# The four transposes of an expert's hidden chunk: from one block ahead of the up products to single ones among them

## The reference, cut to what matters

```
def expert_block(args):
    xb, e = args
    return (jax.nn.silu(xb @ w_gate[e]) * (xb @ w_up[e])) @ w_down[e]
```

## Time and profile before

| what | value |
|---|---|
| median of 3 runs | 1530.83 us (1530.35 to 1530.88) |
| the profiled execution's own time | 1531.03 us |
| its span | 1528.9 us |
| PE busy | 1507.9 us, 99% |
| DVE busy | 1261.7 us, 83% |
| ACT busy | 1096.9 us, 72% |
| first and last turn of a chunk | 581.4 us and 1508.0 us |

### The profile page before, as it was taken

How to read it: one execution, slowest core, us unless ns; L and a number is a source line. 1 busy time by engine, 2 the same in 40 slices (tenths; PEclk the granted TensorE clock), 3 DMA queues, 4 the chain that set the end, 5 groups by cost and what they waited for, 6 DMA issues and landing times.

```text
span 1528.9 us, 22186 instructions
## 1 busy us (share of the span) xinstructions
PE 1507.9 (99%) x7296; PEld 1202.8 (79%) x7296; DVE 1261.7 (83%) x1554; ACT 1096.9 (72%) x1379; POOL 25.2 (2%) x21
## 2 busy tenths in 40 slices
PE   8999999999999999999999999999999999999997
PEld 7778888888877777778778777777777777777775
DVE  5568676666577669999999999999999999999997
ACT  6565555555567648788788888878788788788885
POOL 0000000000000000000000000000000000000000
PEclk9999999999999989999999999999999999999999
DMA  9534374555545479999999999999999999999970
GB/s 339 188 113 137 130 254 166 206 205 190 183 162 183 150 275 368 384 368 380 389 374 376 382 376 371 377 387 366 381 392 358 383 390 355 389 389 356 403 274 30
DMA packets 193224, 454.00 MB, mean 297 GB/s; under 512 B 8176, under 2 KB 12144, under 8 KB 192912
## 3 DMA queue, kind: packets, MB, share of 16 engines
q1 hardware_dynamic: 190560, 443.72, 78.6%
q0 software_dynamic: 2608, 9.57, 2.3%
HBM read 447.37 MB, written 5.90 MB: 296 GB/s over the span
## 4 chain that ended last, share of the span: by engine, by line
PE 95%; DVE 2%; ACT 1%; issue 1%; DMA 0%; SPq 0%; ACTq 0%; DVEq 0%
PE bank L296 26%; PE bank L298 26%; PE bank L297 25%; PE bank L1475 6%; PE bank L1477 3%; PE bank L1996 1%; PE bank L366 1%; DVE w_lo L309 1%; PE bank L794 1%; PE bank L1450 0%; PE bank L1296 0%; PE bank L783 0%; PE bank L1764 0%; PE bank L1771 0%; PE bank L1287 0%
## 5 line engine op out<-in xcount | busy, mean ns | idle before, releaser
L309 DVE TENSOR_TENSOR w_lo<-ring_low,w_hi 128x1024 fp32r<-128x1024 f32 (+2 forms) x442 | 532.7, 1216 | 91.1 <-ACT w_hi L305 64.2
L305 ACT ACTIVATE w_hi<-ring_low 128x1024 fp32r<-128x1024 f32 (+2 forms) x442 | 465.6, 1055 | 137.2 <-PE bank L298 129.0
L309 DVE TENSOR_TENSOR w_lo<-ring,w_hi 128x1024 fp32r<-128x1024 f32 x336 | 404.8, 1222 | 40.0 <-ACT w_hi L305 19.4
L305 ACT ACTIVATE w_hi<-ring 128x1024 fp32r<-128x1024 f32 x336 | 354.8, 1062 | 83.3 <-PE bank L298 83.2
L296 PE MATMUL bank<-w_hi,xe_hi 128*128 128x512 f32 x896 | 353.7, 395 | 0.0
L298 PE MATMUL bank<-w_hi,xe_lo 128*128 128x512 f32 x896 | 349.7, 390 | 0.0
L297 PE MATMUL bank<-w_lo,xe_hi 128*128 128x512 f32 x896 | 348.8, 389 | 0.0
L298 PEld LDWEIGHTS bank<-w_hi,xe_lo 128*128 128x128 f32 x896 | 168.2, 188 | 36.0
L296 PEld LDWEIGHTS bank<-w_hi,xe_hi 128*128 128x128 f32 x896 | 168.3, 188 | 34.7
L297 PEld LDWEIGHTS bank<-w_lo,xe_hi 128*128 128x128 f32 x896 | 168.4, 188 | 34.2
L296 PE MATMUL bank<-w_hi,hT_hi 128*96 128x512 f32 x448 | 177.2, 395 | 0.0
(11 more groups left out here) (308 smaller groups left out, 1650.8 us busy)
## 6 DMA issues: line engine op xcount, KB each, us to landing
ring<-m_gate_dram SPq DMA_DIRECT2D x72, 1024.0 KB, 5.4
ring_low<-m_down_dram SPq DMA_DIRECT2D x72, 1024.0 KB, 6.1
ring<-m_up_dram SPq DMA_DIRECT2D x56, 1024.0 KB, 5.5
ring_low<-m_up_dram SPq DMA_DIRECT2D x56, 1024.0 KB, 6.1
ring_low<-m_gate_dram SPq DMA_DIRECT2D x40, 1024.0 KB, 5.7
ring<-m_down_dram SPq DMA_DIRECT2D x40, 1024.0 KB, 5.4
ring_low<-f_gate_dram SPq DMA_DIRECT2D x14, 1024.0 KB, 5.2
ring_low<-f_up_dram SPq DMA_DIRECT2D x14, 1024.0 KB, 6.1
```

Source lines behind the costliest of these rows:

```text
L305: nc.scalar.activation(w_hi[:, buf, 0:width], src, ACT.Copy).then_inc(hi_ready, 1)
L309: nc.vector.tensor_tensor(w_lo[:, buf, 0:width], src, f32(w_hi[:, buf, 0:width]), ALU.subtract).then_inc(split_ready, 1)
```

## The change

The four transposes of `turn(c-1)` no longer stand between the gate and the up products of chunk c. `gate_up("u", c, q, turned=True)` places one behind each of the first four values of k, that is behind the 3rd, 6th, 9th and 12th matmul of the item, and the fourth counts `h_banked` up. The two waits of `turn` stand ahead of the first up product, with the same values. `turn` itself remains for chunk 6. That makes 6 turns in each of 8 experts, 48 in all, with 192 transposes; 8 turns stay as they were.

```
+            def turn_block(c, j):
+                return nc.tensor.transpose(pb[6][:, j * PLACES:j * PLACES + PLACES], eh[c % 2][:, j * P:j * P + P],
+                                           const("ident")[0:PLACES, 0:PLACES])
+
-            def gate_up(kind, c, q, units=slice(0, 4)):
+            def gate_up(kind, c, q, units=slice(0, 4), turned=False):
                 bank = pb[2 * (c % 2) + (kind == "u")]
+                if turned:
+                    pe.wait_ge(e_prod, 7 * q + (c + 1))
+                    if c > 1:
+                        pe.wait_ge(hT_lo_done, 7 * q + (c - 1))
                 for m, u, n, buf in m_units((kind, c))[units]:
...
                         ins = mm3(bank, xe_hi[:, k, :], xe_lo[:, k, :], w_hi[:, buf, w], w_lo[:, buf, w],
                                   k == 0, k == KD - 1)
+                        if turned and k < 4:
+                            block = turn_block(c - 1, k)
+                            if k == 3:
+                                block.then_inc(h_banked, 1)
                     ins.then_inc(unit_used, 1)
...
                     gate_up("g", c, q)
-                    turn(c - 1, q)
...
-                    gate_up("u", c, q)
+                    gate_up("u", c, q, turned=True)
```

More of the change, by code:

```diff
@@ L1995, in turn @@
                 for j in range(4):
-                    ins = nc.tensor.transpose(pb[6][:, j * PLACES:j * PLACES + PLACES], eh[c % 2][:, j * P:j * P + P],
-                                              const("ident")[0:PLACES, 0:PLACES])
+                    ins = turn_block(c, j)
                 ins.then_inc(h_banked, 1)
```

## The result

The changed kernel takes 1575.93 us (median of 4 runs, 1575.22 to 1576.4), the kernel before 1530.86 us in the same series (4 runs, 1530.35 to 1531.31). The ratio is 1.0294 with a 95% interval of 1.0282 to 1.0307. The forecast was 1575.

A forecast was written before the change was run, and what follows sets the result against it. PE, busy for 99%, was taken as the bound, with ACT and DVE feeding it through four buffers. 1531.03 + 42.2 (transposes and hand-over) + 2.2 (later waits) = 1575.4, stated as 1575 us, range 1560 to 1592.

The forecast's parts named there:

- Part 1: PE's up item: each single transpose costs 0.12 us, four 0.48 instead of the block's 0.36; 5.8 us in all.
- The rival by which the next load would be pulled ahead of the transpose: PE's weight loads: each single transpose costs only 0.04 us, time 1563 us; chance 0.10.
- Part 2: Turned chunk's hand-over from PE to ACT and DVE: PE waits 0.76 us before down; with transposes 0.88 a turn, 42.2 us.
- E: Moment in each turn when the gate item ends and the next product could start on PE; forecast times count from it.
- Part 3: Later waits on DVE's work, at the picks, `turn(LAST)` and the last expert: together 2.2 us.
- the rival that would have kept it at 1.34: DVE's "d" units stay at ACT's pace, 1.34 us apart instead of 1.13: 14 us more, 1589 us; chance 0.10.
- The 0.4 us of the picks: Chunk 1 of seven experts: picks ahead of DVE's next gate unit make PE lose 0.06 us each, 0.4 in all.
- The rivals of the other side: Hand-over to ACT covered: 1537 us, or 1522 if both weight loads of each transpose also hide; chance 0.03 each.
- the third rival: Hand-over to ACT: its late start is absorbed, only the transposes' 0.12 us a turn stays, 1537 us; chance 0.03.

The follow-up runs named there:

- single_gate: Changed kernel with its four single transposes moved from the up item to behind the last four k of the gate item: 1537.41 us, ratio 1.0044.
- block_k3: Changed kernel with the four transposes as one block again, behind the fourth k of the up item: 1568.75 us, ratio 1.0248.
- reorder: Changed kernel with ACT and DVE taking the first "d" unit ahead of their work on the turned chunk: 1537.83 us, ratio 1.0047.
- pair_gate: Changed kernel with the transposes moved to the gate item, two behind k = 5 and two behind k = 7: 1534.16 us, ratio 1.0021.
- block_k1: Changed kernel with the four transposes as one block behind the second k of the up item: 1531.31 us, ratio 1.0003.
- block_k2: Changed kernel with the four transposes as one block behind the third k of the up item: 1535.88 us, ratio 1.0033.
- block_down: Kernel before with the block of chunks 1 to 5 moved ahead of the last unit of the preceding down item: 1528.53 us, ratio 0.9984.

## Why the prediction was right

**What bounds the kernel.** PE at 99% with ACT and DVE behind four buffers was the right picture: the feed has little reserve, and its slack was 1.34 us a chunk. The sweep of the block over k = 1, 2 and 3 (0.4, 5.0 and 37.9 us above the kernel before) brackets that number.

**Part 1, the price of a single transpose.** Taken as 0.12 us from the fourth of the block, between the bounds 0.04 and 0.23. In the changed kernel 853.23 - 852.66 - 0.455 gives 0.115, single_gate's rows give 0.115, and the mean over the 192 single transposes of the changed kernel is 0.123. single_gate's whole loss is 6.5 us for a forecast of 5.8. The rival by which the next load would be pulled ahead of the transpose, at 0.04 and 1563 us, falls with that: the load starts at 852.89, together with the transpose. The Trainium skill, page "TensorE: Matmul & The Clock Gate", section "Step-by-step: what each phase is for", says that weight loads are pulled ahead of matmuls in flight; the traces here show it for one matmul ahead and no further.

**Part 2, the hand-over.** Step by step, from E = 849.77, forecast and found: fourth transpose 3.09 and 3.12; ACT's copy 3.38 and 3.40; first "d" unit on ACT 4.23 and 4.26; on DVE 5.32 and 5.35; PE's record in front of the down item 6.60 (6.54 + 0.06) and 6.63. The second down matmul starts at 856.71, so the first streamed from 856.48, where PE could have gone on at 855.75: 0.73 us for a forecast of 0.76. The next turn's fourth transpose starts at 870.59, 17.70 us behind this one's, as foretold against 16.8; block_k3 and reorder show the two parts apart, 38 us of waits and 7 us of transposes, which add up to 45. Over all 48 turns PE's start-to-start wait in front of the down item is 0.75 us in the mean (0.71 to 0.83).

**Part 3, what is late next.** DVE's four "d" units took 4.63 us, (4.63 - 1.22) / 3 = 1.14 apart, so DVE caught up, and the rival that would have kept it at 1.34 falls. `turn(LAST)` waits for the product 8 times as expected (2.4 us of idle weight load, 0.3 each). By the starts of its products PE loses 0.07 us there in each of seven experts, for a forecast of 0.13, and 0.72 once in the last expert, for a forecast of 0.8. The 0.4 us of the picks did not come: the gate items behind them start within 0.01 us of their time. So this part was somewhat too large in its terms.

**The rivals of the other side** needed slack in the hand-over that was not there: reorder shows that the price of the transposes alone, the 1537 of the third rival, is what comes out when the slack is made.

**What was off** is small, and in part it cancels. The sum came to 44.4 us, the spans differ by 45.4. By the starts in the two traces, 0.9 us of that lies ahead of the experts, where nothing was changed. In the stage of the experts it is 44.7 us: 35.9 of waits in front of the down items (forecast 36.5), 7.0 of transposes (forecast 5.8), 1.8 of the rest (forecast 2.2). The term that was too small is the price of the single transposes: from second matmul to second matmul, as counted for pair_gate, one of them adds 0.128 us in the mean and not 0.12.

## What to carry to other kernels

When a producer's signal is moved later, look at what stands behind the consumer's wait in its own queue: here ACT's wait of 2.2 us for a copy that nobody wanted yet held up the weight unit that PE wanted first. Compare the delay with the slack from that unit's readiness to its use. Here the move was free below it (block_k1), each further 0.68 us was paid in every turn above it (block_k2 to block_k3), and putting the urgent unit ahead of the wait in the queues gave it back (reorder). A transpose cost here what went with the weight load behind it, so four of them were cheapest in one block, in front of the narrower weights.

## What the runs showed of the hardware

A transpose of 96 columns costs PE 0.08 us in front of another one, 0.10 in front of a product with weights of 128 x 96, and 0.12 in front of one with 128 x 128, though its own record is about 0.25 us long in every case. Its own weight load is free behind a matmul of 512 columns: in the changed kernel it starts at 852.66 and the transpose at 852.89, one slot of 0.23 later. Not expected: the gate and up products behind a transpose run late by up to 0.02 us for each k, over the next one to three of them, 0.04 us a turn in the kernel before. This lies in no transpose and in no wait, and it accounts for most of the 1.3 us each by which pair_gate and block_down missed their expectations.
